# Units, turns and the inverse's turns of an RWKV-7 core in TensorE products of 128 stationary columns, with the order of steps written anew

## The reference, cut to what matters

```python
def rwkv7_recurrence(r, decay, k, v, a, b):
    """S_t = S_{t-1} diag(w_t) + (S_{t-1} a_t) b_t^T + v_t k_t^T ;  y_t = S_t r_t."""
    def step(S, inp):
        r_t, w_t, k_t, v_t, a_t, b_t = inp
        sa = jnp.einsum('bhij,bhj->bhi', S, a_t)
        S = S * w_t[:, :, None, :] + sa[..., None] * b_t[:, :, None, :] + v_t[..., None] * k_t[:, :, None, :]
        y = jnp.einsum('bhij,bhj->bhi', S, r_t)
        return S, y
```

## Time and profile before

| | |
|---|---|
| median of the runs | 2597.88 us |
| the profiled execution | 2603.71 us, span 2602.0 us |
| granted TensorE clock over the span | 0.977 |
| PE busy | 2529.3 us (97%) |
| DVE, ACT, POOL busy | 820.0, 935.1, 984.5 us |
| chunks of the recurrence, first to last | about 595 to 838 us of the span |

### The profile page before, as it was taken

One profiled execution on the slowest core, in us unless ns is written; L12 is line 12 of the kernel. 1 busy time (PEld: TensorE's weight loads), 2 busy tenths in 40 slices (PEclk: granted clock), 3 DMA queues, 4 the chain that ended last, 5 costly groups with the idle time before them and its releaser, 6 DMA issues.

```text
span 2602.0 us, 46767 instructions
## 1 busy us (share of the span) xinstructions
PE 2529.3 (97%) x18850; PEld 2120.8 (82%) x18850; DVE 820.0 (32%) x1269; ACT 935.1 (36%) x1556; POOL 984.5 (38%) x470
## 2 busy tenths in 40 slices
PE   8999999998888999999999999999999999999998
PEld 6888886777776788888899998888889777788887
DVE  5222015455553332210432012221043566322200
ACT  4222223634554343321433233332143565333321
POOL 4444442332222354444434444444444101444442
PEclk9999999998898999999999999999999998999999
DMA  4333231210000233322234443332232241333221
GB/s 155 97 97 97 97 105 53 78 42 4 4 4 20 82 105 97 97 97 97 97 122 139 144 142 101 97 97 94 96 118 81 66 128 52 97 96 95 96 96 62
DMA packets 181773, 230.37 MB, mean 89 GB/s; under 512 B 16408, under 2 KB 119992, under 8 KB 181624
## 3 DMA queue, kind: packets, MB, share of 16 engines
q1 hardware_dynamic: 181624, 228.20, 27.5%
HBM read 213.47 MB, written 14.68 MB: 88 GB/s over the span
## 4 chain that ended last, share of the span: by engine, by line
PE 84%; issue 11%; POOL 2%; ACT 1%; DVE 1%; DMA 0%; SPq 0%; POOLq 0%; ACTq 0%; DVEq 0%
PE bank L343 19%; PE bank L345 19%; PE bank L344 19%; PE bank L350 6%; PE bank L352 6%; PE bank L351 6%; POOL w_lo L318 2%; PE bank L1231 1%; PE bank L1344 1%; PE bank L1314 1%; PE bank L1362 1%; PE bank L1790 1%; PE bank L1546 1%; PE bank L1448 1%; PE bank L1266 0%
## 5 line engine op out<-in xcount | busy, mean ns | idle before, releaser
L318 POOL TENSOR_TENSOR w_lo<-w_raw,w_hi 128x1024 fp32r<-128x1024 f32 x376 | 905.1, 2411 | 1342.0 <-ACT w_hi L313 1341.3
L313 ACT ACTIVATE w_hi<-w_raw 128x1024 fp32r<-128x1024 f32 x376 | 395.3, 1058 | 1031.3 <-PE bank L345 861.4
L343 PE MATMUL bank<-xg_hi,w_hi 128*128 128x512 f32 x1408 | 549.7, 390 | 6.6 <-POOL w_lo L318 5.2
L344 PE MATMUL bank<-xg_lo,w_hi 128*128 128x512 f32 x1408 | 547.8, 389 | 0.0
L345 PE MATMUL bank<-xg_hi,w_lo 128*128 128x512 f32 x1408 | 547.8, 389 | 0.0
L343 PEld LDWEIGHTS bank<-xg_hi,w_hi 128*128 128x128 f32 x1408 | 264.3, 188 | 64.3 <-issue 5.4
L345 PEld LDWEIGHTS bank<-xg_hi,w_lo 128*128 128x128 f32 x1408 | 264.3, 188 | 55.4
L344 PEld LDWEIGHTS bank<-xg_lo,w_hi 128*128 128x128 f32 x1408 | 264.3, 188 | 55.3 <-issue 0.7
L343 PE MATMUL bank<-hid_hi,w_hi 128*128 (+1 forms) x704 | 274.4, 390 | 0.0
L344 PE MATMUL bank<-hid_lo,w_hi 128*128 (+1 forms) x704 | 273.9, 389 | 0.0
L345 PE MATMUL bank<-hid_hi,w_lo 128*128 (+1 forms) x704 | 273.9, 389 | 0.0
(11 more groups left out here) (287 smaller groups left out, 3111.9 us busy)
## 6 DMA issues: line engine op xcount, KB each, us to landing
w_raw<-in_ffn_w_in SPq DMA_DIRECT2D x352, 256.0 KB, 3.0
w_raw<-in_ffn_w_out SPq DMA_DIRECT2D x176, 256.0 KB, 2.8
w_raw<-in_w_kv SPq DMA_DIRECT2D x96, 256.0 KB, 3.1
w_raw<-in_rwkv_w_rkv SPq DMA_DIRECT2D x48, 256.0 KB, 2.8
w_raw<-in_attn_w_q SPq DMA_DIRECT2D x48, 256.0 KB, 3.1
k_dram<-stage SPq DMA_DIRECT2D x6, 1024.0 KB, 4.5
v_dram<-stage SPq DMA_DIRECT2D x6, 1024.0 KB, 5.5
keys<-k_dram SPq DMA_DIRECT2D x24, 256.0 KB, 3.5
```

What stands on the lines that cost most here:

```text
L313: act.activation(w_hi[:, s, :], w_raw[:, s, :], ACT.Copy).then_inc(w_hi_ready, 1)
L318: pool.tensor_tensor(w_lo[:, s, :], w_raw[:, s, :], w_hi[:, s, :].bitcast(F32), ALU.subtract).then_inc(w_lo_ready, 1)
L343: pe.matmul(o, hi, x_hi, start=start, stop=False)
L344: pe.matmul(o, hi, x_lo, start=False, stop=False)
```

## The change

The stationary operand of three kinds of products becomes 128 columns wide, with 64 rows as before:

- `un_pe` takes b and k of a head as one stationary operand: 2 steps of 8 instructions a pair, each step filling both work banks. `tp_pe` does the same for the turns to tokens: 16 instructions a pair. The layouts of `units` and `btok`/`ktok` (now `tok`) follow, and so do their masks (`uv_dve`, four a pair as before) and copies.
- So that the result of one head has b above k and of the other k above b, the two factors of the second head swap places in `bk`. POOL now makes the factors of the first head (64 partitions) and DVE those of the second, in two instructions `bkx_dve` a pair that are new on DVE.
- `flip_pe` takes the `inv_x` of two chunks of a head at once: 8 instructions a level.
- `lift` and `join` keep their number and shape; their tiles are renamed.
- `ORDER` is written anew. In it `gp`, `ytp`, `bvp`, `ysb` and others belong to the pair two behind.

```diff
 ORDER = """
-    open+0.0 gs+0.5 yhi-2.0 amb+1.0 ub+1.1 join+0.5 xs+0.5 uk+1.0 yt-1.0 amb+1.1 flip+0.5 amk+1.0 uk+1.1 inv+0.5
...
+    open+0.0 xs+0.5 zs+0.0 bkx+1.1 flip+0.5 odd+1.0 inv+0.5 yvar-2.0 un+1.0 u+0.0 uv+1.0 us+0.0 root-2.0 s+0.0
...
-        def unit_products(pe, q, w, n, which):
-
-            work_free(pe, q, w)
+        def un_pe(pe, q, n):
+            need(pe, "ar", q)
+            need(pe, "bk", q)
+            need(pe, "bx", q)
+            for hh in range(2):
+                work_free(pe, q, f"un{2 * n + hh}")
             for c in range(4 * n, 4 * n + 4):
                 for hh in range(2):
-                    last = pe.matmul(work_bank(q, w)[head(hh if which == 0 else 1 - hh), c % 4 * P:(c % 4 + 1) * P],
-                                     bk[head(hh), q % 2, c, which, :], ar[head(hh), 2 - q % 3, c, :, :], start=True, stop=True)
-            last.then_inc(work_done, 1)
+                    last = pe.matmul(work_bank(q, f"un{2 * n + hh}")[:, c % 4 * P:(c % 4 + 1) * P],
+                                     bk[head(hh), q % 2, c, :, :].rearrange("p w t -> p (w t)"), ar[head(hh), 2 - q % 3, c, :, :],
+                                     start=True, stop=True)
+                    if c % 4 == 3:
+                        last.then_inc(work_done, 1)
...
+        def tp_pe(pe, q, _):
...
+            for c in range(NC):
+                for hh in range(2):
+                    last = pe.matmul(work_bank(q, f"tok{hh}")[:, c * CH:(c + 1) * CH],
+                                     bk[head(hh), q % 2, c, :, :].rearrange("p w t -> p (w t)"), ident2[head(hh), :],
+                                     start=True, stop=True)
...
+        def factors(engine, q, hh, src, slot):
+
+            return engine.tensor_tensor(bk[head(hh), q % 2, :, slot, :], chunks(src[head(hh), :]),
+                                        ucum[head(hh), :, 1:CH + 1], ALU.mult)
+
...
+        def bkx_dve(dve, q, n):
+            need(dve, "scan", q)
+            work_full(dve, q - 2, "un3", "tok1")
+            if n == 0:
+                need(dve, "kka", q)
+                done(factors(dve, q, 1, ta, 1), "bx")
+            else:
+                need(dve, "kp", q)
+                done(factors(dve, q, 1, k_all[:, q], 0), "bx")
...
@@ flip_pe
-            for v, cc, hh in level_tiles():
-                g = 1 - hh if v == 1 else hh
-                src = ident2[head(hh), :]
-                if l > 0:
-                    src = src.rearrange("p (k e r) -> p k e r", e=2, r=1 << l)[:, :, 1, :]
-                last = pe.matmul(bank[2 + v][head(g), cc * n:(cc + 1) * n], inv_x[head(hh), v, cc * CH:(cc + 1) * CH], src,
-                                 start=True, stop=True)
+            for cc in range(4):
+                for hh in range(2):
+                    src = ident2[head(hh), :]
+                    if l > 0:
+                        src = src.rearrange("p (k e r) -> p k e r", e=2, r=1 << l)[:, :, 1, :]
+                    last = pe.matmul(bank[2 + hh][:, cc * n:(cc + 1) * n], inv_x[head(hh), cc, :, :].rearrange("p v t -> p (v t)"), src,
+                                     start=True, stop=True)
```

More of the change, by code:

```diff
@@ new lines @@
+    uv+1.1 state+0.0 un+1.1 z+0.1 decay+0.1 uv+1.2 zs+0.1 u+0.1 uv+1.3 us+0.1 s+0.1 lift+1.0 tp+1.0 state+0.1
+    decay+0.2 gs+1.0 z+0.2 xs+1.0 ynorm-2.0 tok+1.0 flip+1.0 tok+1.1 ytp-2.0 zs+0.2 inv+1.0 u+0.2 ys-2.0 lift+1.1
+    bvp-2.0 gs+1.1 us+0.2 yt-1.0 s+0.2 join+1.1 bv-1.0 state+0.2 decay+0.3 z+0.3 xs+1.1 zs+0.3 ysb-2.0 u+0.3
+    flip+1.1 ysum-1.0 zwza+2.0 us+0.3 inv+1.1 s+0.3 ycen-1.0 lift+1.2 tw+2.0 state+0.3 z+0.4 gs+1.2 join+1.2
+    decay+0.4 xs+1.2 kkp+2.0 dec+2.0 flip+1.2 zs+0.4 pscan+2.0 u+0.4 inv+1.2 pscan+2.1 lift+1.3 us+0.4 ta+2.0 s+0.4
@@ L972, in rwkv_project_dve @@
                     arr_dve(dve, 0, 0)
+                    for n in range(2):
+                        bkx_dve(dve, 0, n)
         def rwkv_project_pe(pe, ph):
@@ L1086, in lev, with unit, own_unit, key_unit @@
             return psum[:, 2:4, 0:n].rearrange("p v (k r) -> p v k r", r=1 << l)
[L1088 to L1092, removed]
+        def unit(q, rows, c, hh, part):
+            return units[rows, 1 - q % 2, c, hh, part * CH:(part + 1) * CH]
+        def own_unit(q, c, hh, part):
+            return unit(q, head(hh), c, hh, part)
+        def key_unit(q, c, hh, part):
+            return unit(q, head(1 - hh), c, hh, part)
         def y_bank(q):
@@ L1264, in btp_pe @@
             for c in range(NC):
                 for hh in range(2):
-                    last = pe.matmul(work_bank(q, "btok")[head(hh), c * CH:(c + 1) * CH], bk[head(hh), q % 2, c, 0, :],
-                                     ident2[head(hh), :], start=True, stop=True)
-            last.then_inc(work_done, 1)
-        def ktp_pe(pe, q, _):
-            need(pe, "bk", q)
-            work_free(pe, q, "ktok")
-            for c in range(NC):
-                for hh in range(2):
-                    last = pe.matmul(work_bank(q, "ktok")[head(1 - hh), c * CH:(c + 1) * CH], bk[head(hh), q % 2, c, 1, :],
-                                     ident2[head(hh), :], start=True, stop=True)
-            last.then_inc(work_done, 1)
@@ L1290, in level_tiles, with tok_act @@
+                    if c == NC - 1:
+                        last.then_inc(work_done, 1)
+        def tok_act(act, q, hh):
+            need(act, "y", q - 2)
+            work_full(act, q, f"tok{hh}")
+            read_work(act.activation(tok[:, q % 2, hh], chunks(work_bank(q, f"tok{hh}")[:, :]), ACT.Copy), q, f"tok{hh}")
         def level_tiles():
@@ L1301, in lift_pe @@
                 need(pe, "inv", q - 1)
-                after_read(pe, q, "ub0")
-                after_read(pe, q, "ub1")
+                for n in range(4):
+                    after_read(pe, q, f"un{n}")
             else:
@@ L1327, in gs_dve @@
                 need(dve, "x_odd", q)
-                out = blocks(inv_x[:, :, :], 0, 0)[:, :, :, 0].rearrange("p v (c k) -> p v c k", c=4)
+                out = inv_x[:, :, :, :].rearrange("p c v (k e) -> p v c k e", e=2)[:, :, :, :, 0]
             else:
@@ L1359, in join_pe @@
             need(pe, "inv", q, l)
-            for v, cc, g in level_tiles():
-                hh = 1 - g if v == 1 else g
-                last = pe.matmul(bank[2 + v][head(hh), cc * 32:(cc + 1) * 32], inv_u[head(g), q % 2, v, cc * CH:(cc + 1) * CH],
-                                 inv_g[head(g), v, cc * 32:(cc + 1) * 32], start=True, stop=True)
+            for cc, v, hh, slot, g in level_tiles():
+                last = pe.matmul(bank[2 + slot][head(hh), cc * 32:(cc + 1) * 32],
+                                 inv_u[head(g), q % 2, hh, cc * CH:(cc + 1) * CH],
+                                 inv_g[head(g), hh, cc * 32:(cc + 1) * 32], start=True, stop=True)
             done(last, "join")
@@ L1408, in open_pe @@
             need(pe, "yt", q - 2)
-            for n in range(2):
-                after_read(pe, q, f"uk{n}")
+            for n in range(4):
+                after_read(pe, q, f"un{n}")
             z_values(pe, q, 0)
@@ L1447, in u_pe @@
                 rows = rows_of(c, hh)
-                last = pe.matmul(u_columns(c)[head(hh), :], inv_u[rows, q % 2, c // 4, c % 4 * CH:(c % 4 + 1) * CH],
+                last = pe.matmul(u_columns(c)[head(hh), :], inv_u[rows, q % 2, hh, c % 4 * CH:(c % 4 + 1) * CH],
                                  zs[rows, :], start=True, stop=True)
```

116 lines of the change are left out of this document (48 added, 68 removed).

## The result

The changed kernel takes 2739.82 us (median of four runs, 2737.74 to 2740.74), the kernel before 2596.73 us beside it: a ratio of 1.054, with a 95% interval of 1.0526 to 1.0554. It is slower by 143 us where 25 were forecast, and outside the range. The profiled execution has a span of 2739.0 us against 2602.0.

What follows compares the result with a forecast made beforehand. PE, 88% busy in the recurrence, was taken to set the pace; +2.65 us a pair at full clock, /0.92 = +2.9, over eight pairs +23, plus 2 for the first pair: 2598 + 25 = 2623 us, range 2587 to 2655 (its own 2608 to 2640).

Steps and rivals of the forecast that it cites:

- the division by 0.92: Carrying the full-clock sum over at the clock of the kernel before: +2.65 us a pair becomes +2.9.
- The sum at full clock: Per pair: units -1.75, turns -0.1, flips +2.5, tile shape +1.7, DVE +0.3, order 0, together +2.65 us.
- some 2: Sign that the steps were right: PE's busy time a pair up by some 2 us despite 80 fewer instructions.
- Changes of tile shape: PE switching between 64*64 and 64*128 products: 0.35 us an excursion, 0.10 us gap at each change, +1.7 us a pair.
- The count of nine: Excursions to 64*128 products a pair after the change, by the order of steps, where there were three before.
- DVE's products: Two new DVE instructions a pair, 2 us of work mostly hidden: +0.3 us a pair, bounds 0 and +1.3.
- The order: New order of steps: shorter passage between pairs, but the work stands in other chunks; taken as 0, bounds -3.8 and +2.9.
- The signs named for it: Signs for the order: passage between pairs at 3.5 us, and chunk 1 at 5 to 6.
- Theory M: From the follow-up runs: lift of level 0 waiting for all four masks in place of two costs; 2615 to 2622 expected.
- Instructions count, not columns: Rival: PE's time goes with instructions, so fewer in units, turns and flips pay; 2568 us, chance 0.10.
- Slack won: Rival: passage between pairs falls from 6 to 3.4 us and moved blocks hide in waits; 2591 us, chance 0.20.
- Long steps on the chain: Rival: flips and turns overhang the gaps behind `u` and `s`, the chain waits; +5.5 a pair, 2646 us, chance 0.17.

Runs made afterwards that it cites:

- d2: Changed kernel with wide flips streaming 128 moving columns and lift and join streaming 64: 2638.12 us, ratio 1.0131.
- b1: Changed kernel with each wide flip streaming its moving columns in copies, 128 in place of 32 or 64: 2640.15 us, ratio 1.0137.
- b2: Kernel before with lift, join and flip streaming their 32 moving columns twice: 2594.65 us, ratio 0.9962.
- b3: Changed kernel with flips, units and turns back at 64 stationary columns, and lift, join and flip streaming their 32 columns twice: 2620.65 us, ratio 1.0056.
- c2: Changed kernel in the old order of steps, flips, units and turns at 64 stationary columns on four tiles in turn: 2638.85 us, ratio 1.0125.
- c3: As c2, with lift, join and flip streaming their 32 columns twice: 2617.37 us, ratio 1.0057.
- c1: Changed kernel's products, all wide, in the order of steps of the kernel before: 2719.09 us, ratio 1.0438.
- c4: As c1, with the wide flips streaming 128 moving columns: 2656.04 us, ratio 1.0219.
- d1: Kernel before with flips of levels 1 to 5 streaming 8 moving columns in place of 32, inverse not computed: 2609.66 us, ratio 1.0022.
- a4: Changed kernel with flips, units and turns all back at 64 stationary columns, four tiles in turn, new order kept: 2652.96 us, ratio 1.0193.
- d4: As c5, but the factors of both heads on POOL as in the kernel before: 2623.77 us, ratio 1.0065.
- c5: As c3, but units and turns on two tiles at a time as in the kernel before: 2621.51 us, ratio 1.0078.

## Why the prediction failed, step by step

**The step that failed is the division by 0.92.** The sum was made at full clock and carried over at the clock of the kernel before, "+2.65 us at full clock, /0.92 = +2.9". The changed kernel has 0.56 there. The clock was mentioned once, as something that "would add" to a rival, without a price. It should have been a rival with its own: in the changed kernel a pair went from 32.16 to 47.9 us, and the eight cost over 100.

**The sum at full clock was near.** Flip 1.08 us for 1.05. A load of 128 columns does follow its forerunner on the same tile at 0.11 us. For units and turns d2 has rows at the full level, 1.16 us for 1.1 and 2.00 for about 2, and a clock of 1.00 over six whole pairs, from chunk 0 of pair 1 to chunk 0 of pair 7:

```profile
641.13:846.01 204.88, 181.84 (x5020) 150.24 (x5016) 114.05 (x233) 94.20 (x251) 42.12 (x36) 1.00 0.01 3
...
675.21 1.16 PE L1257 MATMUL bank<-ar,bk 64*128 64x128 f32 x16 [0.49 <-DVE units L1269]
679.04 2.00 PE L1281 MATMUL bank<-ident,bk 64*128 64x64 f32 x32
```

That is 34.15 us a pair, where the kernel before took 30.86 in its pair at full clock: +3.3, and +2.65 was forecast. PE is busy for 30.3 us a pair in place of 28.4, "some 2" more, as was said. The changed kernel can't be read this way: its 10.2 us at full level and 37.6 at half come to 29.0 us of full clock, fewer than before (32.16 x 0.92 = 29.6), since what PE waits for on other engines takes no longer at half its clock (`us` takes ACT 0.22 us in both kernels). That is what makes the miss instructive: the sum counted what PE is *occupied* with, and was about right in it, and the clock went by something else.

**What moved the clock, as far as the runs show.** PE was busy 29.89 of 31 us while the clock stood at 0.50. So it wasn't idleness as the busy share counts it. A load of 128 columns with 32 moving columns behind it keeps its tile occupied for 0.11 us and streams for a quarter of it (an estimate: 512 columns stream for 0.42 us, so 32 for 0.026). Where only the number of moving columns was raised (b1, b2, b3, c2 to c3, c1 to c4), the clock rose each time, by 0.05 to 0.41. Where it was lowered (d1), it fell by 0.06. The runs give the direction and no rule for how much. Whether the tiling matters as well is open: a4 and c2 pack units and turns into half the time and have a clock below that of the kernel before until their streams are doubled, but they differ from it in more than the tiles.

The Trainium skill says, in "TensorE: Matmul & The Clock Gate", section Part 1: The HAM clock gate, that the gate is set by how busy PE has been lately, and its table in "Why this matters for your kernels" warns of idle gaps between bursts of matmuls. Read with the busy share of the profile, that forecasts a clock no worse than before, and the trace disagrees: busier, with 1.1 of 31 us idle, and at the half level.

**Changes of tile shape.** The 0.10 us gap was right (the second record of L1169 starts at 734.52 + 1.12 - 0.59 = 735.05 and streams 0.42, the flip follows at 735.57). That change, from 16*128 to 64*128, lies inside what the prediction counted as one excursion. The count of nine fits the trace, which has 53 runs of 64*128 products in six pairs. What they cost isn't isolated by a run.

**DVE's products:** +0.3 a pair was forecast, 0.2% of the time in all; d4 against c5 (1.0065 against 1.0078) tells it neither from nothing nor from twice as much.

**The order:** taken as 0. With fed flips it won 16 us for wide products (c4 against b1), in part by the clock. The signs named for it came: in b1 the passage between pairs is 3.55 us in the mean of pairs 1 to 6, and 6.06 before, and from chunk 1 to 2 it takes 6.60, and 3.51 before. What the passage gave back was paid in the chunks. Behind the last `us` the order costs 5 to 8 us (b1, the changed kernel, d2), which the prediction had not looked at: in the changed kernel the output projection starts 7.7 us later.

**What is left with fed flips.** With fed flips 35 us over the kernel before remain, and +25 was the forecast. By the timeline of b1 (first `us` at 611.28, last at 869.51) 16 us lie ahead of the first `us`, 12 between first and last, 5 behind. The part ahead is pair 0's inverse with no chunks to hide behind, and most of it is the clock again: from 555 us to the first `us` it is 0.64 over 56.28 us in b1 and 0.79 over 40.05 before, 36.0 and 31.6 us at full clock, so some 12 of the 16 (an estimate). Feeding lift and join didn't mend that (d2, 0.65). Where it was mended the start came earlier: in b3 the first `us` is at 598.0 us, and at 607.1 in a4. The prediction had spread this part evenly over the pairs. Without the 12, b1 is some 23 us over the kernel before; that this meets the +25 is in part luck, since b1's pairs ran at a higher clock than those before, and the 5 us behind were not in the sum.

**Theory M was not in the prediction.** That the lift must wait for all four masks stands in the changed kernel (`for n in range(4): after_read(pe, q, f"un{n}")`), and only the loads and streams of the unit step were priced.

**The rivals.** "Instructions count, not columns" fell: 80 fewer a pair, and slower. "Slack won" fell: the passage shrank as it said, and a pair at full clock is longer all the same (34.15 for 30.86). "Long steps on the chain" forecast 2646 and +5.5 a pair; at full clock +3.3 was measured, between the sum and this rival, and chunk 1 is where it said.

## What to carry to other kernels

Before making small float32 products wider, compare each tile's load with its stream. If the load is the longer one, fewer instructions won nothing here, and the array was granted less clock; the price of a lost clock is all PE-bound work in the stretch, not only the changed step. Read the granted clock by stretch first and ask of a change what it does to streaming, not to busy time. Where a product is bound by its load, extra moving columns cost next to nothing (0.08 us a flip here) and can pay: 0.4% of the kernel before, 3.6% of the changed one.

## What was not expected of the hardware

- PE busy 96% (29.89 of 31 us), and the clock at its half level through all of it; and a kernel 100 us faster because it streams up to four times as many columns in its flips, copies that nobody reads.
- The clock's pattern was the same four times behind each other: 37.5 us at half, 10.2 at full. What PE did around one rise (727.9) and one fall (738.1), from its timeline: turns with 64 moving columns, on two tiles, behind each other, then the mixed steps of a chunk with 512-column products, and at the fall a lift and a join with 32 (the rows at 737.23 and 738.43 above):

```profile
725.15 1.65 PE L1551 MATMUL bank<-ident,yt 64*64 64x64 f32 x26
...
727.05 1.02 PE L1317 MATMUL bank<-inv_x,units 64*64 64x32 f32 x30
727.91 0.95 PE L1551 MATMUL bank<-ident,bv 64*64 64x64 f32 x26
```
